# Residual hand-overs tile by tile, last weight pieces in another order, inner tiles split early, modulation sums as columns

## The reference

```python
def rms_norm(x, g):                    # per token over its 1024 features
    return x * lax.rsqrt(jnp.mean(x * x, axis=-1, keepdims=True) + EPS) * g

# block 1
hn = rms_norm(h, mix_norm_pre);     # to retention and attention
h = h + rms_norm(mixed @ w_out, mix_norm_post)
hn = rms_norm(h, ffn_norm_pre)
up = causal_dwconv(hn @ w_up, conv_w, conv_b); g, u = split(up, 2)
h = h + rms_norm((silu(g) * u) @ w_down, ffn_norm_post)

# block 2, layer 0 (HGRN mixer) and layer 1 (NSA attention with its own shared keys and values)
mods = silu(c) @ ada_w + ada_b                           # four modulations, each of 3 x 1024 sums
shift, scale, gate = split(mods[2 * layer], 3)
x = x + gate * mixer(rms_norm_2(x, norm_mix) * (1 + scale) + shift)
shift, scale, gate = split(mods[2 * layer + 1], 3)
x = x + gate * swiglu(rms_norm_2(x, norm_ffn) * (1 + scale) + shift, ffn_w_in, ffn_w_out)
```

## Time and profile before

| | |
|---|---|
| median of 3 runs | 2380.25 us (2379.84 to 2380.41) |
| the profiled execution | 2381.53 us, span in the trace 2379.8 |
| busy PE | 2143.7 us, 90% of the span |
| busy DVE | 1295.1 us, 54% |
| busy ACT | 793.7 us, 33% |
| busy POOL | 125.6 us, 5% |

### The profile page before, as it was taken

One profiled execution on the slowest core, in us unless ns is written; L12 is line 12 of the kernel. 1 busy time (PEld: TensorE's weight loads), 2 busy tenths in 40 slices (PEclk: granted clock), 3 DMA queues, 4 the chain that ended last, 5 costly groups with the idle time before them and its releaser, 6 DMA issues.

```text
span 2379.8 us, 28136 instructions
## 1 busy us (share of the span) xinstructions
PE 2143.7 (90%) x10760; PEld 1734.0 (73%) x10760; DVE 1295.1 (54%) x2205; ACT 793.7 (33%) x1379; POOL 125.6 (5%) x100
## 2 busy tenths in 40 slices
PE   3998896999898799999899999799579988999997
PEld 3876575888787688887787878679456657888786
DVE  2479447788653524673655564564576854222334
ACT  2333434333323435122422222333246533222221
POOL 0002301000000110000000000100201100000000
PEclk8999898999999899999999999899689879999999
DMA  4321123556342132102456553223200122233221
GB/s 145 107 71 54 36 72 97 185 172 200 116 164 84 62 105 91 36 1 71 145 165 206 166 180 121 80 76 106 73 1 2 37 95 78 93 97 98 89 97 45
DMA packets 146641, 233.08 MB, mean 98 GB/s; under 512 B 7276, under 2 KB 83532, under 8 KB 146252
## 3 DMA queue, kind: packets, MB, share of 16 engines
q1 hardware_dynamic: 142304, 222.28, 28.7%
q10 hardware_dynamic: 3340, 5.85, 0.7%
q0 software_dynamic: 864, 3.15, 0.4%
HBM read 229.16 MB, written 2.10 MB: 97 GB/s over the span
## 4 chain that ended last, share of the span: by engine, by line
PE 80%; DVE 11%; issue 3%; ACT 3%; POOL 2%; DMA 1%; ACTq 0%; DVEq 0%; POOLq 0%
PE ps L1919 10%; PE ps L1921 10%; PE ps L1920 10%; PE ps L1941 5%; PE ps L1942 4%; PE ps L1943 4%; PE ps L1888 4%; PE ps L2176 4%; PE ps L1889 4%; PE ps L1890 4%; PE ps L2093 4%; PE ps L2095 3%; PE ps L1958 3%; PE ps L1983 2%; PE ps L1970 2%
## 5 line engine op out<-in xcount | busy, mean ns | idle before, releaser
L1348 DVE TENSOR_TENSOR w_lo<-ring,w_hi 128x1024 fp32r<-128x1024 f32 (+4 forms) x362 | 376.3, 1042 | 785.9 <-ACT w_hi L882 784.9
L882 ACT ACTIVATE w_hi<-ring 128x1024 fp32r<-128x1024 f32 (+4 forms) x362 | 329.3, 912 | 978.9 <-PE ps L1921 460.4
L1919 PE MATMUL ps<-x_hi,w_hi 128*128 128x512 f32 x1056 | 415.1, 393 | 0.3 <-DVE w_lo L1348 0.3
L1920 PE MATMUL ps<-x_lo,w_hi 128*128 128x512 f32 x1056 | 411.0, 389 | 0.0
L1921 PE MATMUL ps<-x_hi,w_lo 128*128 128x512 f32 x1056 | 411.0, 389 | 0.0
L1919 PEld LDWEIGHTS ps<-x_hi,w_hi 128*128 128x128 f32 x1056 | 198.2, 188 | 50.6 <-DVE w_lo L1348 8.7
L1920 PEld LDWEIGHTS ps<-x_lo,w_hi 128*128 128x128 f32 x1056 | 198.3, 188 | 42.0 <-issue 1.4
L1921 PEld LDWEIGHTS ps<-x_hi,w_lo 128*128 128x128 f32 x1056 | 198.2, 188 | 41.7
L1941 PE MATMUL ps<-w_hi,x_hi 128*128 128x512 f32 x528 | 207.7, 393 | 15.6 <-DVE x_hi L1408 15.6
L1942 PE MATMUL ps<-w_lo,x_hi 128*128 128x512 f32 x528 | 206.8, 392 | 0.0
L1943 PE MATMUL ps<-w_hi,x_hi 128*128 128x512 f32 x528 | 206.7, 391 | 0.0
(11 more groups left out here) (291 smaller groups left out, 3181.9 us busy)
## 6 DMA issues: line engine op xcount, KB each, us to landing
ring<-in_ada_w SPq DMA_DIRECT2D x48, 1024.0 KB, 5.1
ring<-in_ffn_w_in SPq DMA_DIRECT2D x88, 512.0 KB, 4.8
ring<-in_w_up SPq DMA_DIRECT2D x44, 512.0 KB, 4.5
ring<-in_ffn_w_out SPq DMA_DIRECT2D x20, 1024.0 KB, 4.9
ring<-in_hgrn_w_in SPq DMA_DIRECT2D x16, 1024.0 KB, 5.2
ring<-in_w_in SPq DMA_DIRECT2D x12, 1024.0 KB, 5.0
ring<-in_w_down SPq DMA_DIRECT2D x10, 1024.0 KB, 4.9
ring<-in_kv_ada_w SPq DMA_DIRECT2D x8, 1024.0 KB, 5.1
```

The lines of the kernel that those rows point to most:

```text
L882: a.activation(to[:, n % depth, 0:src.shape[-1]], src, ACT.Copy).then_inc(s["hi_done"], 1)
L1348: v.tensor_tensor(to[:, n % depth, 0:width], src, hi[:, n % depth, 0:width].bitcast(F32), ALU.subtract).then_inc(s["lo_done"], 1)
L1919: mm(bs[j], wh[:, k, c], x_hi[:, 2 * q + k], start=first, stop=False)
L1920: mm(bs[j], wh[:, k, c], x_lo[:, 2 * q + k], start=False, stop=False)
```

## The change

1. Hand-overs go tile by tile, and an instruction of its own loads ACT's table of the square root ahead (`sqrt_table`). ACT squares straight out of the banks, one half at a time, and takes a square root for each tile; DVE weights, scales, adds and normalises tile by tile (`y_weighted`, `y_added`, `x_normed`, and `gated`, `gated_added` at stages 2 to 5). POOL adds nothing any more. The PE takes the transposes of the first four feature tiles as each token tile arrives, and the other 16 at the end.
2. The last two weight pieces of a mixer's second half and of down are multiplied in an order in which token tile 0 is complete earlier (`LAST_ORDER`, pairs of piece and tile).
3. `hid` tiles 0 and 1 are split into a buffer of their own (`hid_early`) ahead of up's last taps and gates.
4. Modulation sums that are needed as columns are made as columns, with four matmuls of one column each. The sums are given other places: two in the first two ups of the third FFN, four in the down of the second, none in or behind the NSA attention.

```diff
-        ADA = [(0, j) for j in range(6)] + [(1, j) for j in range(6)] + [(2, j) for j in range(6)] \
-            + [(4, j) for j in range(4)] + [(3, j) for j in range(6)]
+        ADA = [(0, j) for j in range(6)] + [(1, j) for j in range(4)] + [(2, j) for j in range(2)] \
+            + [(1, 4), (1, 5)] + [(2, j) for j in range(2, 6)] + [(4, j) for j in range(4)] + [(3, j) for j in range(6)]
-        ada_after.update({(1, u): [ADA[12 + u]] for u in range(11)})
-        ada_down = {0: ADA[10:12], 1: ADA[23:25]}
-        ADA_LATE = ADA[25:]
+        ada_after.update({(1, u): [ADA[12 + u]] for u in range(10)})
+        ada_after.update({(2, u): [ADA[26 + u]] for u in range(2)})
+        ada_down = {0: ADA[10:12], 1: ADA[22:26]}
+        ADA_ROWS = [mj for mj in ADA if mj not in ada_down[0] + ada_down[1]]
...
+        hid_early = over("hid_early", [P, 4, S], KT * S + 17408)
+
+        def hid_parts(k):
+
+            if k < 2:
+                return hid_early[:, k], hid_early[:, 2 + k]
+            return x_hi[:, k % 4], x_hi[:, 4 + k % 4]
...
+        LAST_ORDER = [(2, 0), (2, 1), (3, 0), (3, 1), (2, 2), (3, 2), (2, 3), (3, 3)]
...
+            def x_rms(i, t):
+
+                if i:
+                    x_part_ready(i - 1, t, 1)
+                step(a.activation(XN[i][:, t], x_tok[:, t], ACT.Square, accum_out=stat[:, t:t + 1]))
+                after()
+                a.activation(stat[:, 4 + t:5 + t], stat[:, t:t + 1], ACT.Sqrt, scale=1.0 / D, bias=eps[:, :]).then_inc(s["norm_rms"], 1)
...
+            def y_square(stage, t, half):
+
+                p = filled(act, part_key(stage, half, t))
+                at = (16, 28)[half] + t
+                step(a.activation(junk[:, 0:HALF], p, ACT.Square, accum_out=stat[:, at:at + 1]))
+                after()
+                if half == 0:
+                    a.activation(stat[:, 12 + t:13 + t], stat[:, at:at + 1], ACT.Identity, scale=1.0 / D, bias=eps[:, :])\
+                        .then_inc(s["y_sq"], 1)
...
+            def post(stage):
+
+                i = stage + 1
+                if i in (2, 4):
+                    early_highs(i, slice(0, 3))
+                if stage < 2:
+                    if stage in HALF_FIRST:
+                        for t in range(NT):
+                            y_square(stage, t, 0)
+                    for t in range(NT):
+                        for half in range(stage in HALF_FIRST, 2):
+                            y_square(stage, t, half)
+                        if t:
+                            x_rms(i, t - 1)
+                    if i not in (2, 4):
+                        early_highs(i, slice(0, 1))
+                    x_rms(i, NT - 1)
+                else:
+                    for half, t in PARTS[stage]:
+                        if (half, t) == (1, NT - 1) and i not in (2, 4):
+                            early_highs(i, slice(0, 1))
+                        x_half_square(i, t, half)
...
+            def x_normed(i, t):
+
+                dve.wait_ge(s["norm_rms"], NT * i + t + 1)
+                step(v.reciprocal(stat[:, 8 + t:9 + t], stat[:, 4 + t:5 + t]))
+                after()
+                v.tensor_scalar(XN[i][:, t], x_tok[:, t], stat[:, 8 + t:9 + t], None, ALU.mult).then_inc(s["xn_ready"], 1)
...
+            def y_weighted(stage, half, t):
+
+                key = part_key(stage, half, t)
+                p = filled(dve, key)
+                f = slice(half * HALF, (half + 1) * HALF)
+                dve.wait_ge(s["y_sq"], 2 * NT * stage + PARTS[stage].index((half, t)) + 1)
+                dve.wait_ge(s["row_in"], 32)
+                v.tensor_tensor(STAGE_Y[stage][:, t, f], p, row[:, stage, f], ALU.mult).then_inc(free(key), 1)
+
+            def y_added(stage, t):
+
+                dve.wait_ge(s["y_sq"], 2 * NT * stage + PARTS[stage].index((1, t)) + 1)
+                step(v.reciprocal(stat[:, 24 + t:25 + t], stat[:, 20 + t:21 + t]))
                 after()
+                for half in range(2):
+                    evacuated(dve, part_key(stage, half, t))
+                v.scalar_tensor_tensor(x_tok[:, t], STAGE_Y[stage][:, t], stat[:, 24 + t:25 + t], x_tok[:, t], ALU.mult, ALU.add)\
+                    .then_inc(s["x_ready_v"], 1)
+
+            def post_norm(stage):
+
+                i = stage + 1
+                if i == 2:
+                    early_lows(i, slice(0, 3))
+                if stage in HALF_FIRST:
+                    for t in range(NT):
+                        y_weighted(stage, 0, t)
                 for t in range(NT):
+                    for half in range(stage in HALF_FIRST, 2):
+                        y_weighted(stage, half, t)
+                    if t >= 1:
+                        y_added(stage, t - 1)
+                    if t >= 2:
+                        x_normed(i, t - 2)
+                y_added(stage, NT - 1)
+                x_normed(i, NT - 2)
+                if stage == 1:
+                    ada_columns(0)
+                x_normed(i, NT - 1)
+                if i != 2:
+                    early_lows(i, slice(0, 1))
...
+            def post_gate(stage, m):
+
+                i = stage + 1
+                if i == 4:
+                    early_lows(i, slice(0, 3))
+                if stage in HALF_FIRST:
+                    for t in range(NT):
+                        gated(stage, m, 0, t)
+                        if t:
+                            gated_added(stage, 0, t - 1)
+                    gated_added(stage, 0, NT - 1)
+                for t in range(NT):
+                    if stage in HALF_FIRST:
+                        gated(stage, m, 1, t)
+                        gated_added(stage, 1, t)
+                    else:
+                        gated(stage, m, 0, t)
+                        gated(stage, m, 1, t)
+                        gated_added(stage, 0, t)
+                        gated_added(stage, 1, t)
+                    if t and stage < 5:
+                        x_normed(i, t - 1)
+                if stage == 3:
+                    ada_columns(1)
+                if stage < 5:
+                    x_normed(i, NT - 1)
+                if i in (3, 5):
+                    early_lows(i, slice(0, 1))
...
+                dst = mod[:, m, 1, 4 * j:4 * j + 4] if j < 2 else mod[:, m, 0, 4 * (j - 2):4 * (j - 1)]
+                ins = v.tensor_tensor(dst, p, vec[:, BIAS + 24 * m + 4 * j:BIAS + 24 * m + 4 * j + 4], ALU.add)
...
-                up_out(i, FFN_UNITS - 1)
+                w = arrived(dve, ("down", i, 0), (0,))
+                low(("down", i, 0), in_halves(w, 2, PIECE)[:, 0, 0])
+                for k in range(2):
+                    hid_low(i, k)
+                up_taps(i, FFN_UNITS - 1, (0, 1, 2, 3))
+                low(("down", i, 1), in_halves(w, 2, PIECE)[:, 0, 1])
+                up_gated(i, FFN_UNITS - 1)
...
-            def late_terms(i):
-
-                n, k = divmod(i - 96, KT)
-                if 0 <= n < 2:
-                    ada_term(*ADA_LATE[n], k)
-
-            attention("nsa", late_terms, nsa_finish)
-            ada_out(*ADA_LATE[0])
-            ada_sum(*ADA_LATE[2])
-            ada_out(*ADA_LATE[1])
-            ada_out(*ADA_LATE[2])
+            attention("nsa", lambda i: None, nsa_finish)
             out_parts(2, "mix3")
-            post_gate(4, 2, y3, tok_keys("mix3"))
+            post_gate(4, 2)
...
             def norm(i):
-                pe.wait_ge(s["xn_ready"], NT * (i + 1))
-                for kt in range(KT):
+                banks = [open_bank(("xT", i, kt)) for kt in range(4)]
+                for t in range(NT):
+                    pe.wait_ge(s["xn_ready"], NT * i + t + 1)
+                    for kt in range(4):
+                        ins = tr(banks[kt][:, t * P:(t + 1) * P], XN[i][:, t, kt * P:(kt + 1) * P], ident)
+                        if t == NT - 1:
+                            ins.then_inc(full(("xT", i, kt)), 1)
+                for kt in range(4, KT):
                     turn(lambda t: XN[i][:, t, kt * P:(kt + 1) * P], ("xT", i, kt))
...
+                if j < 4:
+                    ada_sums(m, j, b).then_inc(full(("ada", m, j)), 1)
+                else:
+                    mm(b, ones[:, :], ada_held(m, j), start=True, stop=True).then_inc(full(("ada", m, j)), 1)
+
+            def ada_sums(m, j, b, at=0):
+
+                for k in range(4):
+                    ins = mm(b[:, at + k:at + k + 1], ada_held(m, j)[:, k * P:(k + 1) * P], ones[:, 0:1], start=True, stop=True)
+                return ins
...
+                steps = [(k, t, half) for k in range(FT - 2) for t in range(NT) for half in range(2)]
+                steps += [(FT - 4 + q, t, half) for q, t in LAST_ORDER[0:4] for half in range(2)]
+                steps += [(FT - 4 + q, t, half) for t in (2, 3) for half in range(2) for q in (2, 3)]
+                for k, t, half in steps:
+                    if (t, half) == (0, 0):
+                        pe.wait_ge(s["lo_done"], n + 1)
```

(21 more changed lines are left out.)

266 lines of the change are left out of this document (134 added, 132 removed).

## The result

| | before | changed |
|---|---|---|
| median | 2380.05 us (2377.16 to 2380.41, 4 runs) | 2307.84 us (2307.61 to 2309.47, 4 runs) |
| ratio, 95% interval | | 0.9701 (0.9684 to 0.9717) |
| profiled execution, span | 2381.53, 2379.8 | 2307.61, 2305.8 |
| busy PE, DVE, POOL | 2143.7, 1295.1, 125.6 | 2135.4, 1261.0, 91.8 |

A forecast was written before the change was run, and what follows sets the result against it. PE was taken as the bound, busy 2143.7 of 2379.8 us, leaving waits and half-clock time to gain. Terms 47.9 + 3.9 - 1.7 + 8.9 + 17 = 76.0 gave a median of 2304.3, range 2294 to 2325.

The forecast's parts named there:

- Hand-overs at stages 0, 1, 2, 4 and norm 0: Scaled tiles reach PE's transposes earlier: gains of 8.3, 13.5, 4.75 and 5.4 us at the stages, 3.2 at norm 0.
- The loop: At stage 0, ACT and DVE alternate square, weighting, addition and root from tile to tile: 4.6 us a tile.
- Stage 3: Hand-over with last tile at T+8.8, T being the end of PE's products ahead of it: gain 8.0 us.
- Stage 5: After PE's last product, DVE's half steps end at T+2.8 (T: end of PE's products) instead of T+7.6: gain 4.7 us.
- PE's stand for the last hid tile: In down, PE stands about 0.55 us for the last piece's small half, taken as already counted in stages 1, 3, 5.
- Start of down: Early split starts FFN0 and FFN1 1.05 and 2.35 us earlier, FFN2 1.0 later; with the clock, gain 3.9, bounds 0 and 6.
- FFN1's wait falls to 2.2, worth another 1.5: Second FFN's start of down: the wait is short enough for the clock to stay, gaining another 1.5 us.
- The direction for the third FFN: FFN2's down starts 1.0 us later, because piece 1's w_lo stands ahead of the operations that free the last banks.
- Modulations: Moved rows cost 1.0 us, two more sums in FFN1's down 0.7, columns instead of rows 0: together -1.7.
- the column's price: In modulation sums, four column matmuls at 0.23 us each take 0.92 on PE, against 1.02 for a row.
- NSA tail and late section: Attention's last groups at full clock gain 17 us; no modulation between attention and mix gains 8.9.
- the largest single bet: In the NSA attention's tail, the clock stays up without DVE's late terms: gain 17 us, bounds 7 and 3.

The follow-up runs named there:

- The transposes' experiment: The changed kernel with PE's transposes of a norm again waiting for all four token tiles: 2319.68 us, ratio 0.9744.
- piece 1's low later: The changed kernel with high and low of down's piece 1 behind up's last gates instead of ahead of them: 2296.49 us, ratio 0.9648.

## Why the prediction was right, point by point

- **Hand-overs at stages 0, 1, 2, 4 and norm 0**: right within 0.6 each, and term by term. The loop was stepped from durations of the earlier trace rows and came out at 4.58 for 4.6. The last tile's transposes gained 7.7, 12.5, 2.9 and 4.1 at stages 0, 1, 2 and 4 (forecast 7.4, 11.9, 3.1, 4.4), and what follows them, with twelve transposes fewer, 1.1, 1.4, 1.8 and 1.3 (forecast 0.9, 1.6, 1.6, 1.0). The transposes' experiment shows that they are on the path; undone alone they cost more than that at stages 0, 2 and 4. The hand-over by tiles itself was not undone in any run.
- **Stage 3** was 1.4 more. The last tile's transposes come at T+7.2 and not T+8.8: DVE's work from the first gate product took 13.8 instead of 14.9, and the 0.8 where it should wait for a bank did not come. The clock worked against it: the last 16 transposes take 3.62 in the changed kernel and 1.91 with piece 1's low later, where the clock had come back before them.
- **Stage 5** was 2.0 more. I took only DVE's last addition. Before, all four stores began from 2370.79 on, and the span ended 4.7 after the last addition; now they begin at 2295.57 and it ends 3.1 after it. That is 1.6, a term left out; that it is the stores' earlier start is argued, no run moves them alone.
- **PE's stand for the last hid tile** in each down: the prediction has it "already in stages 1, 3 and 5", but their working counts from T on both sides and this stand comes ahead of T, so it was taken as nothing. It is a wait of 0.51 and a first product of 0.47, 0.68 a down, 2.0 in all. Stages 3 and 5, both under-forecast, hide it in the sum.
- **Start of down**: the term that failed, 3.9 against -0.2. The first two FFNs start 0.7 and 1.3 earlier for 1.05 and 2.35, and for another reason than forecast: it is the cheap columns; the early split itself made all three waits longer while PE waited for all eight banks, as undoing it shows (4.7 us faster). The step "FFN1's wait falls to 2.2, worth another 1.5" gave 3.23 and a first product of 0.62, and behind the wait of 3.90 in the third FFN the clock was at half too, 1.6 that I hadn't counted. The direction for the third FFN was right and its cause is shown: with low of piece 1 moved, the wait is 1.15 and the product takes 0.47.
- **Modulations**: -1.0 for -1.7; the column's price was right.
- **NSA tail and late section**: 25.7 for 25.9. That the clock stays up was the largest single bet, and putting DVE's terms back undoes it. That the sum is so close is partly luck: the four groups gave 15.9 for 17.7 (a group takes 5.7, not 5.3), and from the last group to the transposes 10.1 came for 8.2; ahead of the four groups 0.6 was lost. The swing that the Trainium skill describes in "TensorE: Matmul & The Clock Gate", "A second HAM failure mode: psum-queue depth-cycling", for a kernel with short idles between its groups of matmuls did not come: PE's idle time in 1846 to 1870 is 0.65 us of 24, and the clock reads 1.00.
- **The total**, 74.0 for 76.0, is closer than its terms: start of down and the last hid tile together fell short by 6.1, stages 0, 1, 3 and 5 gave 4.4 more.
